# A hybrid decoder step on one core: the output gates' stage, with softmax shares spread by a 0/1 product and cached values moved in four column groups

## The reference, cut to what matters

```
def _combine_groups(outs, lses):
    w = jax.nn.softmax(jnp.stack(lses, axis=0), axis=0)
    return jnp.einsum('gbth,gbthd->bthd', w, jnp.stack(outs, axis=0))
```

```
p = jnp.exp(s - lse[..., None])
outs.append(jnp.einsum('bthj,btjhd->bthd', p, kvg[:, :, :, 1]))
```

## Time and profile before

| what | value |
|---|---|
| median of three runs | 2349.15 us |
| the profiled execution, its own time | 2345.67 us |
| its span, first to last instruction | 2343.9 us |
| mean granted TensorE clock | 0.976 |
| TensorE (PE) busy | 2239.1 us, 96% |
| VectorE (DVE), ScalarE (ACT), GpSimd (POOL) busy | 960.4, 507.4, 675.8 us |
| the stage `output_gates` in the span | about 1120 to 1283 us |

### The profile page before, as it was taken

The page is one execution under the profiler, slowest core; times in us unless marked ns, Lnnn a source line. Parts: engine busy times, 40 slices in busy tenths (PEclk is TensorE's granted clock), DMA queues, the critical chain, the costliest instruction groups (busy, mean ns, idle before and its releaser), DMA issues. The chain is left out here.

```text
span 2343.9 us, 34455 instructions
## 1 busy us (share of the span) xinstructions
PE 2239.1 (96%) x13918; PEld 2098.1 (90%) x13918; DVE 960.4 (41%) x1817; ACT 507.4 (22%) x1108; POOL 675.8 (29%) x662
## 2 busy tenths in 40 slices
PE   5899999999999989999798989889999999999999
PEld 4678999999877779999798989889999999999998
DVE  5765773575133412333352642434332233333224
ACT  3311553454232213333111010221000000000001
POOL 4224112232132223221230223534433223443310
PEclk9999999999999999999888889999999999999999
DMA  6426244444467746553774662523332223332202
GB/s 220 140 95 200 97 156 149 164 158 154 140 227 250 243 134 203 188 187 129 198 243 160 202 218 95 185 59 121 108 90 86 67 83 117 108 108 90 86 32 73
DMA packets 206636, 337.78 MB, mean 144 GB/s; under 512 B 45158, under 2 KB 117670, under 8 KB 203782
## 3 DMA queue, kind: packets, MB, share of 16 engines
q1 hardware_dynamic: 141624, 269.49, 35.6%
q10 hardware_dynamic: 64854, 66.10, 8.9%
HBM read 262.55 MB, written 161.04 MB: 181 GB/s over the span
## 5 line engine op out<-in xcount | busy, mean ns | idle before, releaser
L273 POOL CAST whi<-raw 128x512 fp32r<-128x512 f32 x324 | 242.5, 748 | 1550.5 <-PE ps L1972 520.4
L275 POOL TENSOR_TENSOR wlo<-raw,whi 128x512 fp32r<-128x512 f32 x324 | 441.1, 1361 | 33.3 <-issue 7.4
L286 PE MATMUL ps<-whi,hhi 128*128 128x512 f32 x832 | 346.6, 417 | 1.4 <-ACT zt L628 0.7
L288 PE MATMUL ps<-whi,hlo 128*128 128x512 f32 x832 | 334.2, 402 | 0.0
L287 PE MATMUL ps<-wlo,hhi 128*128 128x512 f32 x832 | 334.0, 401 | 0.0
L1972 PE MATMUL ps<-h2hi,whi 128*128 128x344 f32 x1056 | 225.3, 322 | 9.8 <-DVE h2lo L2527 8.3
L286 PEld LDWEIGHTS ps<-whi,hhi 128*128 128x128 f32 x832 | 208.4, 251 | 21.7 <-ACT zt L628 1.2
L288 PEld LDWEIGHTS ps<-whi,hlo 128*128 128x128 f32 x832 | 208.4, 250 | 20.8
L287 PEld LDWEIGHTS ps<-wlo,hhi 128*128 128x128 f32 x832 | 209.6, 252 | 18.9
L1972 PE MATMUL ps<-h2lo,whi 128*128 128x344 f32 x1056 | 224.5, 321 | 0.0
L1972 PE MATMUL ps<-h2hi,wlo 128*128 128x344 f32 x1056 | 223.9, 320 | 0.0
(11 more groups left out here) (312 smaller groups left out, 3371.4 us busy)
## 6 DMA issues: line engine op xcount, KB each, us to landing
out<-in_cache_kv_w SPq DMA_DIRECT2D x144, 512.0 KB, 4.8
raw<-in_w_in SPq DMA_DIRECT2D x152, 256.0 KB, 4.4
a_tr<-tt SPq DMA_DIRECT2D x48, 256.0 KB, 2.0
out<-in_cache_kv_w SPq DMA_DIRECT2D x24, 508.0 KB, 5.0
raw<-in_w_gate SPq DMA_DIRECT2D x88, 128.0 KB, 2.2
raw<-in_w_up SPq DMA_DIRECT2D x88, 128.0 KB, 2.4
raw<-in_w_down SPq DMA_DIRECT2D x44, 256.0 KB, 3.7
gates<-e_sg ACTq DMA_DIRECT2D x16, 516.0 KB, 4.8
```

What stands on the lines that cost most here:

```text
L273: pool.tensor_copy(self.whi[:, p % RING, :], self.raw[:, p % RAW, :]).then_inc(self.w_hi, 1)
L275: pool.tensor_tensor(self.wlo[:, p % RING, :], self.raw[:, p % RAW, :], self.whi[:, p % RING, :].bitcast(F32), ALU.subtract).then_inc(self ...
L286: nc.tensor.matmul(out, lhs[0], rhs[0], start=start, stop=False)
L288: return nc.tensor.matmul(out, lhs[1], rhs[0], start=False, stop=stop)
```

## The change

`GroupMerge`: the way through DRAM goes. VectorE rounds the shares to a high part `ch` (fp32r) and keeps the rest as a low part, and puts both into `cc` (for each token tile 96 columns: 3 groups of 32, of which 16 are used). TensorE turns it at i = 4 with 8 transposes, ScalarE copies the result to `ct` (96 x 1024, fp32r) at i = 5. A 0/1 matrix `pick`, made by VectorE at i = 0, is now stationary (16 rows by 128 columns); the tokens of `ct` move, taken in the group's order by a strided view (`residues`: step 1, 4 and 8 for the three groups). A tile is 4 matmuls in place of 8.

`SampleSoftmax`: the cached values now move (128 columns) and 32 columns of weights stand; each of the 4 pairs of heads has its own 32 rows of PSUM, that is its own column group of the array. After the last row ScalarE copies both banks, TensorE turns them with 8 transposes after segment 20, and VectorE's last step moves from i = 19 to i = 20. GpSimd waits at the stage's start for the deferred stores of the stages before.

```
@@ GroupMerge.__init__
-        self.cr = sb("cr", [P, G, NT, H], ctx=c)
+        self.ch = sb("ch", [P, G, NT, H], F32R, c)
+        self.ct = sb("ct", [self.ROWS, S], F32R, c)
+        self.pick = sb("pick", [self.ROWS, H, DH], F32R, c)
+        self.cc = self.at[:, 0, 0:NT * self.ROWS].rearrange("p (n r) -> p n r", n=NT)
@@ act
-        elif i == 4:
-            act.wait_ge(self.c_done, 1)
-            for g in range(G):
-                act.dma_start(core.cf_nat[g].rearrange("(n p) c -> p n c", p=P), self.cf[:, g]).then_inc(self.c_out, 16)
         elif i == 5:
-            act.wait_ge(self.c_out, 16 * G)
-            for g in range(G):
-                for dst, src in by_tile(self.cr[:, g], core.cf_nat[g], g):
-                    act.dma_start(dst, src).then_inc(self.c_in, 16)
+            act.wait_ge(self.c_tr, 1)
+            act.activation(self.ct[:].rearrange("p (a c) -> p a c", a=2), core.ps[0:self.ROWS, 2:4, :],
+                           ACT.Copy).then_inc(self.c_t, 1)
@@ dve
+        if i == 0:
+            ch.mark(dve.memset(self.cc, 0.0))
+            ch.link(dve.memset(self.pick[:].bitcast(F32), 0.0))
+            for g in range(G):
+                rows = slice(32 * g, 32 * g + 2 * H)
+                high, low = (bc(core.ident[rows, 32 * g + x:32 * g + x + H], [2 * H, H, DH]) for x in (0, H))
+                dve.tensor_tensor(self.pick[rows], high, low, ALU.add).then_inc(self.picks, 1)
...
+            ch.link(dve.tensor_copy(self.ch[:], cf[:]))
+            ch.link(dve.tensor_tensor(cf[:], cf[:], self.ch[:].bitcast(F32), ALU.subtract))
+            parts = self.cc.rearrange("p n (g x h) -> p g x n h", g=G, h=H)
+            for g in range(G):
+                for x, part in enumerate((self.ch[:].bitcast(F32), cf)):
+                    dve.tensor_copy(parts[:, g, x], part[:, g]).then_inc(self.c_done, 1)
@@ pe
+        if i == 4:
+            pe.wait_ge(self.c_done, 2 * G)
+            for n in range(NT):
+                last = pe.transpose(ps[0:self.ROWS, 2 + n // 4, n % 4 * P:(n % 4 + 1) * P], self.cc[:, n, :],
+                                    core.ident[:])
+            last.then_inc(self.c_tr, 1)
...
+            rows = slice(32 * g, 32 * g + 2 * H)
+            share = residues(self.ct[:], g, n)[rows]
             for j in range(4):
-                for two in range(2):
-                    share = self.cr[:, g, n, 2 * j + two:2 * j + two + 1].to_broadcast([P, DH])
-                    last = pe.matmul(ps[DH * two:DH * two + DH, 2 + u % 2, j * P:(j + 1) * P], share, core.ident[:],
-                                     start=True, stop=True)
+                heads = self.pick[rows, 2 * j:2 * j + 2, :].rearrange("p h c -> p (h c)")
+                last = pe.matmul(ps[:, 2 + u % 2, j * P:(j + 1) * P], heads, share, start=True, stop=True)
@@ SampleSoftmax.act
+        elif i == self.END:
+            act.wait_ge(self.pv, NB)
+            for a in range(2):
+                act.activation(self.ov[:, 4 * a:4 * a + 4, :].rearrange("p b c -> p (b c)"), core.ps[:, 7 - a, :],
+                               ACT.Copy).then_inc(self.ove, 1)
@@ SampleSoftmax.pe
-            for j in range(4):
-                for g in range(G):
-                    at = (b * 4 + j) * 2
-                    last = pe.matmul(ps[:, 7, at:at + 2], self.vc[:, b % 2, g, j * P:(j + 1) * P],
-                                     ss[:, b, g, 2 * j:2 * j + 2], start=(g == 0), stop=(g == G - 1))
+            if b == NB // 2:
+                pe.wait_ge(self.lr, 1)
+            flat = ss[:].rearrange("p b g h -> p (b g h)")
+            for g in range(G):
+                for j in range(4):
+                    at = (b * G + g) * H + 2 * j
+                    last = pe.matmul(ps[self.W * j:self.W * j + self.W, 7 - b // 4, b % 4 * P:(b % 4 + 1) * P],
+                                     flat[:, at:at + self.W], self.vc[:, b % 2, g, j * P:(j + 1) * P],
+                                     start=(g == 0), stop=(g == G - 1))
             last.then_inc(self.pv, 1)
+        elif i == self.END + 1:
+            pe.wait_ge(self.ove, 2)
+            for b in range(NB):
+                last = pe.transpose(ps[:, 4 + b // 4, b % 4 * P:(b % 4 + 1) * P], self.ov[:, b, :], ident[:])
+            last.then_inc(self.otp, 1)
@@ output_gates
         def _(pool):
+            core.settle(pool)
             parts[1][0].pool()
```

More of the change, by code:

```diff
@@ L1152 @@
 class GroupMerge:
+    ROWS = 32 * G
     FIRST = 6
@@ L1245, in pe @@
         core, pe, ps = self.core, self.core.nc.tensor, self.core.ps
-        if i == self.FIRST:
-            pe.wait_ge(self.c_in, 16 * sum(len(by_tile(self.cr[:, g], core.cf_nat[g], g)) for g in range(G)))
+        if i == 4:
[4 more added lines that the diff above has]
+            last.then_inc(self.c_tr, 1)
+        elif i == self.FIRST:
+            pe.wait_ge(self.picks, G)
+            pe.wait_ge(self.c_t, 1)
         for u in self.pair(i):
@@ L1647 @@
     END = 4 + NB
+    W = 32
     def __init__(self, core, c):
@@ L1662, in __init__ @@
         self.zs = sb("s_z", [NB, G, 512], ctx=c)
-        (self.z_in, self.dgd, self.bcp, self.amx, self.sub, self.ex, self.vtp, self.lp, self.pv, self.done,
-         self.out) = (sem(f"s_{x}") for x in ("zin", "dg", "bcp", "amx", "sub", "ex", "vtp", "lp", "pv", "done", "out"))
+        self.ov = self.vc[:, 0, 0:2, :].rearrange("p a (b c) -> p (a b) c", c=P)
+        (self.z_in, self.dgd, self.bcp, self.amx, self.sub, self.ex, self.vtp, self.lp, self.lr, self.pv, self.ove,
+         self.otp, self.done, self.out) = (sem(f"s_{x}") for x in ("zin", "dg", "bcp", "amx", "sub", "ex", "vtp", "lp", "lr",
+                                                                  "pv", "ov", "otp", "done", "out"))
         self.v_in = [sem(f"s_vin{i}") for i in range(2)]
@@ L1697, in pool @@
     def pool(self):
-        flat = lambda a: a[:].rearrange("p b g h -> p (b g h)")
+        flat = lambda a: a[:, 0:NB].rearrange("p b g h -> p (b g h)")
         self.core.nc.gpsimd.partition_all_reduce(flat(self.sa), flat(self.core.ss), P,
@@ L1706, in dve @@
         if i == 0:
+            ch.link(dve.memset(ss[:, NB:], 0.0))
             sn = core.sn[:].rearrange("b g h -> b (g h)")
@@ L1723, in dve @@
             dve.wait_ge(self.lp, 1)
-            ch.link(dve.tensor_tensor(flat(sa), ps[:, 6, 0:C], flat(nw), ALU.add))
+            ch.wait()
+            dve.tensor_tensor(flat(sa), ps[:, 6, 0:C], flat(nw), ALU.add).then_inc(self.lr, 1)
+            dve.wait_ge(self.lr, 1)
             ch.link(dve.tensor_reduce(ll[:], sa[:].rearrange("p b g h -> p b h g"), AX.X, ALU.add))
@@ L1736, in dve @@
             ch.link(dve.tensor_tensor(vt[:, 0], vt[:, 0], vt[:, 2], ALU.add))
-        elif i == self.END:
+        elif i == self.END + 1:
             ot = self.ot
-            dve.wait_ge(self.pv, NB)
+            dve.wait_ge(self.otp, 1)
             for two in range(2):
                 rows = slice(DH * two, DH * two + DH)
-                src = ps[rows, 7, 0:NB * H].rearrange("p (b j two) -> p two j b", two=2, j=4)[:, two]
+                src = ps[rows, 4:6, :].rearrange("p a (b j c) -> p j (a b) c", j=4, c=self.W)[:, :, :, two]
                 ch.mark(dve.tensor_tensor(ot[rows], vt[rows, 0], src, ALU.add))
@@ L1761, in pe @@
             pe.wait_ge(self.ex, 2)
-            pe.matmul(ps[:, 6, 0:C], core.ones[:], ss[:].rearrange("p b g h -> p (b g h)"),
+            pe.matmul(ps[:, 6, 0:C], core.ones[:], ss[:, 0:NB].rearrange("p b g h -> p (b g h)"),
                       start=True, stop=True).then_inc(self.lp, 1)
@@ L2558, in program @@
             core.front(ch)
-            core.ss = core.sb("ss", [P, NB, G, H], ctx=ch)
+            core.ss = core.sb("ss", [P, NB + 2, G, H], ctx=ch)
             core.sn = core.sb("sn", [NB, G, H], ctx=ch)
```

17 lines of the change are left out of this document (8 added, 9 removed).

## The result

The changed kernel took 2320.22 us in the median of four runs (2319.06 to 2327.14), the kernel before 2348.2 beside it. The ratio is 0.9885, 95% interval 0.9869 to 0.99: 27 us faster (23 to 31). I had forecast 15 us and a range that ended at 2323. The direction was right and the size was not.

The account below looks back on a forecast made before the run. TensorE, busy 96% of the span, was taken as the bound. Terms 1.5 - 3.4 + 0.1 - 7.2 + 1.1 - 7.7 + 0.8 = -14.8 us gave 2330.9 or 2334.4, stated as 2332.5 us, range 2323 to 2344.

Parts of the forecast that it names:

- The pairs of groups 1 and 2: Pairs at i = 10 and 13 to 17: stepped moving tokens make them 2.19 and 2.35 us, 0.10 and 0.26 dearer.
- the rivals with 0.13: Step costs nothing on the moving side: those pairs fall to 1.23 us, 6.4 us more gain, near 2326; chance 0.13.
- My own sign of being wrong: Wrong if cached rows take over 2.7 us, pairs of all groups cost the same, or the low clock remains.
- The cached rows: 24 records 55 ns apart make a row 1.65 us, not 2.68; seven rows from 1200.57 us on give -7.2 us.
- This rival: Column groups run beside each other in cached rows: seven rows at 1.0 us, 4.6 us more gain, near 2328; chance 0.12.
- The draining rival: Column groups do not pipeline: a cached row takes 6.5 us, kernel 22 us slower, near 2369; chance 0.08.
- Group 0's pairs: Pairs at i = 6 to 9: 112 ns a matmul, 1.23 us a pair, together -3.4 us.
- The wait at i = 4: TensorE waits 3.0 us for VectorE's shares; with transposes and 2.26 us of old waits gone, +1.5 us.
- Gain lost behind segment 12: First cached row's 1.03 us (i = 11) and pairs of 11 and 12 become longer VectorE wait, counted as zero.
- The clock: From 1200.57 to 1265.82 us the low clock costs 9.6 us; 1.9 left for one fall, so -7.7 us.
- The end: Eight transposes after segment 20, with their fill, cost +0.8 us.
- the two faster rivals: Step free on the moving side (near 2326, chance 0.13) and column groups beside each other (near 2328, chance 0.12).

Follow-up runs that it names:

- the shares' run: Changed GroupMerge with the old SampleSoftmax, against the kernel before: ratio 1.0008 (0.9994 to 1.0021).
- the two-later runs: Changed kernel with VectorE's sums chain at i = 19 and GroupMerge two segments later, run twice: ratios to the kernel before 0.9861 and 0.9867.
- the late-sums run: Changed kernel with VectorE's chain of the sums moved from i = 11 to i = 19: ratio to the kernel before 0.988 (0.9858 to 0.9901).
- The last experiment on the rows: Kernel before, its old cached rows moving and writing 128 columns in place of 2: ratio to the kernel before 0.9969 (0.9955 to 0.9982).

## Why the prediction was right or wrong

- **The pairs of groups 1 and 2: wrong, the step that failed most.** I "charge[d] the moving side the same, as it is the same memory", 233 and 253 ns a matmul. They are 130 and 123 ns apart in the mean. Two errors: the moving side pays half of what the load pays for a step of 4 (0.45 against 0.95 ns an element), and I added it to the 112 ns of the load, where it runs beside the load and only the larger of the two counts. Mis-sized: the five pairs from i = 13 on, +1.1 forecast, 5 x (1.08 - 2.09) = -5.1 us measured. The bounds in the text had held this (1.23 us a pair), and it stood among the rivals with 0.13. My own sign of being wrong, that pairs of all groups cost nearly the same, is what came.
- **The cached rows: right in kind, mis-sized.** 24 records at 55 ns were forecast, 26 ns measured; the row costs 0.98 us and not 1.65. Seven rows: -11.9 us against -7.2. The step that failed is the price of a record: I took the 55 ns of the old pairs for what a record with a short load costs. They are 109 ns for two records, one in each half of the columns, side by side; four side by side make 27, and 24 x 0.027 + 0.33 = 0.98 us. I wrote that no row separated overlap from a short load, but the trace of before did, in the single records of a pair. This rival had 0.12; the "near 1.0 us" that I drew for it from a factor of 2.38 follows from neither 55 ns (0.88) nor 112 (1.46). The draining rival, slower by 22 us, is out.
- **Group 0's pairs: right.** 5.00 us from pair to pair, less 3.77: 1.23 us, as forecast, with the load setting the pace.
- **The wait at i = 4: wrong by 3 us.** VectorE was done at 1149.24, and TensorE came at 1150.12 with no wait. GpSimd was waiting for a transfer from 1147.6 to 1150.3, and VectorE's last eight operations ran undisturbed: the six small ones, which I had put at 0.36 us each, lasted 0.19 and started 0.10 apart. The five before them took 4.1 us in place of 5.4. In the shares' run GpSimd was splitting again from 1145.77 on, three of the six lasted 0.63 to 1.26 us, and TensorE waited 1.58 us; in the two-later runs it waited 3.47 and 4.01. In the six profiles of the changed kernel, as it is or with only its rows, its steps or its sums altered, it did not wait. It is a race whose outcome the trace of before does not fix.

```profile
1149.05 0.19 DVE L1241 COPY at<-cf 128x64 f32<-128x64 f32 x1
1150.34 0.61 POOL L272 CAST whi<-raw 128x512 fp32r<-128x512 f32 x1 [2.75 <-DMA raw<-in_w_in]
```

```profile
1146.56 1.26 DVE L1241 COPY at<-ch 128x64 f32<-128x64 f32 x1
```

- **Gain lost behind segment 12: right, too small.** The wait grew by 5.0 us. That the stretch came out 1.5 us longer, not 0.1, is VectorE's: from the sigmoid of segment 10 to the second tile of segment 12 it took 18.84 us in place of 17.39, and of its four additions on the way (L1254, before L1242) three took 2.05 to 2.11 us beside GpSimd, where before one did. The fallen clock only kept the 0.4 us that the shorter tile would have given (1.05 us from it to the row, 0.64 at full clock in the late-sums run).
- **The clock: right.** At full clock the stretch after it would be 7 x 0.98 + 7 x 3.77 + 5 x 1.08 = 38.7 us; it took 41.8. The low clock and one short wait for cached values (0.22 us) cost 3.1 where it had been 9.6: -6.5, -7.7 forecast. The last experiment on the rows shows the cause.
- **The end: right,** +0.9 against +0.8.

The two mis-sized terms (-6.2 and -4.7), the wait (-2.9) and the smaller ones (+1.4, +1.2, +0.1, -0.2) make, but for rounding, -11.2, the distance from -14.8 to -26.0. The chances were drawn up as if the two faster rivals excluded each other. Both held. Their two gains from my own 2332.5 make 2321.5, already below the 2323 at which I ended the range as "near" them, and with the wait they lie further past it.

## What to carry to other kernels

When a matmul's operands trade places, price load and stream apart and take the larger: a stepped read that doubles the stream costs nothing as long as it stays under the load. When a trace gives a mean distance for small outputs in separate parts of the columns, look at the single records before using it as a price: here it was one distance of 109 ns shared by as many records as there were parts in turn, and only the order that takes all parts in turn reaps it. And look at what moves in a thin stretch before shortening its neighbours: where the clock falls, a shortened neighbour can buy nothing at all, and more columns moved in the same time can make the kernel faster.

## What the runs showed of the hardware that was not expected

- 32-bit matmul records of 128 moving columns, at a granted clock of 1.00, follow 109 ns apart within one column group, with 32 columns loaded as with 64; four groups in turn start four records within 20 ns and so come to 26 ns a record, two halves to 55.
- A step of 4 elements on the moving operand of the rounded format doubles the time of a column (0.456 to 0.90 ns), and beside a load of 128 columns it is all but hidden (118 ns a matmul in place of 112). On a load it costs 0.95 ns an element more.
- 24 matmuls that load 128 columns each take the same 2.7 us with 2 and with 128 moving columns, but after the first kind the granted clock fell to the 1.2 GHz level (9.4 us of the stage, 7 us of the kernel), after the second it did not.
- Shortening the matmuls next to that stretch made the low clock last longer: 14.9 us of cost in place of 9.6.
